# Block 1 in two groups of 256 tokens, the second computed in the expert slots of tiles 0 and 1

## The reference

```python
mod = (cond @ w_ada[l] + b_ada[l]).reshape(b, 6, d)
hn = modulate(rmsnorm(x, norm1_g[l]), shift1, scale1)
proj = hn @ w_in[l]
ya = dsa_attention(...)              # top 128 of the causal keys by an index score, softmax
yb = stick_breaking_attention(...)   # A[t,s] = beta_ts * prod_{s<j<t}(1-beta_tj), s < t
merged = sigmoid(ga) * (ya @ w_proj_a[l]) + sigmoid(gb) * (yb @ w_proj_b[l])
x = x + gate1[:, None, :] * (merged @ w_out[l])
hn2 = modulate(rmsnorm(x, norm2_g[l]), shift2, scale2)
# experts: top 16 of 128 x 128 sums of two key scores, for each token and head
pre = einsum('cd,chkd->chk', hc, u[ec]); coef = gc * gelu(pre)
f = einsum('chk,chkd->cd', coef, v[ec])
x = rmsnorm(x + gate2[:, None, :] * f, final_g)
x = second_block(x, meta_tokens_2, ...)
```

## Time and profile before

| | us |
|---|---|
| median of 3 runs (lowest, highest) | 2416.7 (2405.41, 2417.39) |
| span of the profiled execution | 2407.7 |
| first expert rows multiplied | 604.5 |
| token tile 0 summed | 939.4 |
| token tile 3 summed | 2032.8 |
| busy PE, DVE, ACT, POOL | 1877.5, 1439.3, 988.3, 574.0 |
| moved by DMA | 712.12 MB, 296 GB/s on average |

### The profile page before, as it was taken

How to read it: one execution, slowest core, us unless ns; L and a number is a source line. 1 busy time by engine, 2 the same in 40 slices (tenths; PEclk the granted TensorE clock), 3 DMA queues, 4 the chain that set the end, 5 groups by cost and what they waited for, 6 DMA issues and landing times.

```text
span 2407.7 us, 37910 instructions
## 1 busy us (share of the span) xinstructions
PE 1877.5 (78%) x14736; PEld 1182.7 (49%) x14736; DVE 1439.3 (60%) x3280; ACT 988.3 (41%) x2352; POOL 574.0 (24%) x554
## 2 busy tenths in 40 slices
PE   5998889999766644444435798988888885999999
PEld 3877457777333311100002453355666553677887
DVE  6747744554877677777777768765444333223554
ACT  3123545523443333333333576844444212343443
POOL 0000000001444444444344334443333331000000
PEclk8999999999887655555556897689999997999999
DMA  8932002233999999999999999999999996313565
GB/s 298 333 98 71 1 29 68 71 108 136 404 419 420 420 420 420 420 420 418 418 417 400 405 411 409 390 418 418 418 417 417 418 418 266 118 54 110 184 182 168
DMA packets 123616, 712.12 MB, mean 296 GB/s; under 512 B 14592, under 2 KB 15744, under 8 KB 57648
## 3 DMA queue, kind: packets, MB, share of 16 engines
q0 software_dynamic: 74608, 542.25, 54.6%
q1 hardware_dynamic: 48592, 167.33, 19.9%
q10 hardware_dynamic: 240, 0.16, 0.0%
HBM read 707.56 MB, written 2.13 MB: 295 GB/s over the span
## 4 chain that ended last, share of the span: by engine, by line
PE 46%; DMA 31%; DVE 10%; ACT 6%; issue 5%; POOL 2%; ACTq 0%; SPq 0%; DVEq 0%
DMA arena<-experts,eidx 30%; PE psum L718 9%; PE psum L719 8%; PE psum L720 8%; PE psum L1017 7%; DVE arena L1975 5%; POOL arena L1945 2%; PE psum L1308 2%; PE psum L1135 2%; ACT arena L1589 1%; PE psum L1185 1%; PE psum L1223 1%; ACT sq L1597 1%; PE psum L1259 1%; PE psum L1062 1%
## 5 line engine op out<-in xcount | busy, mean ns | idle before, releaser
L1975 DVE CUSTOM_DVE_ANT_0 arena<-arena 128x1024 f32<-128x1024 f32 x560 | 679.5, 1223 | 412.0 <-DMA arena<-experts,eidx 371.0
L1017 PE MATMUL psum<-arena,sq 32*32 32x512 f32 x8192 | 445.4, 842 | 449.4 <-ACT sq L1597 340.7
L1945 POOL DMA_INDIRECT arena<-experts,eidx x512 | 560.8, 1095 | 947.6 <-PE psum L1017 778.5
L1017 PEld LDWEIGHTS psum<-arena,sq 32*32 32x32 f32 x8192 | 95.1, 120 | 694.6 <-ACT sq L1597 500.5
L1583 ACT ACTIVATE arena<-arena 128x2 f32<-128x2 f32 x256 | 52.0, 203 | 736.5 <-DVE arena L1975 722.1
L718 PE MATMUL psum<-hn_high,w_high 128*128 128x512 f32 (+1 forms) x416 | 176.2, 424 | 15.4 <-DVE hn_low L1972 15.4
L720 PE MATMUL psum<-hn_high,ring_low 128*128 128x512 f32 (+1 forms) x432 | 175.2, 405 | 0.0
L719 PE MATMUL psum<-hn_low,w_high 128*128 128x512 f32 (+1 forms) x416 | 170.4, 410 | 0.0
L1330 PE MATMUL psum<-n_t,ring 128*128 128x256 f32 x704 | 164.3, 389 | 1.1 <-DVE n_t L1972 1.1
L1330 PEld LDWEIGHTS psum<-n_t,ring 128*128 128x128 f32 x704 | 132.5, 192 | 48.7 <-issue 30.1
L1597 ACT ACTIVATE sq<-sq,arena 128x32 f32<-128x32 f32 x512 | 136.9, 313 | 23.8
(11 more groups left out here) (327 smaller groups left out, 3102.1 us busy)
## 6 DMA issues: line engine op xcount, KB each, us to landing
ring<-w_stream SPq DMA_DIRECT2D x262, 512.0 KB
arena<-w_ada SPq DMA_DIRECT2D x48, 512.0 KB, 6.3
arena<-experts,eidx POOLq DMA_INDIRECT x512
arena<-cum_rows POOLq DMA_DIRECT2D x1, 2112.0 KB, 9.7
x<-xT SPq DMA_DIRECT2D x1, 2048.0 KB, 12.6
arena<-rel_rows POOLq DMA_DIRECT2D x1, 2048.0 KB, 15.3
arena<-sub_keys POOLq DMA_DIRECT2D x1, 1024.0 KB, 5.8
outT<-hn_rest SPq DMA_DIRECT2D x8, 128.0 KB
```

The costliest lines, as they stand in the source:

```text
L1017: last = mm(bank(4 + 2 * odd + a)[QUART * b:QUART * b + QUART, :], diag[k, s, :], rows[k, s, D + a * 512:D + (a + 1) * 512], start=c == 0, ...
L1945: nc.gpsimd.indirect_dma_start(rows[:, s, :], None, experts, bass.IndirectOffsetOnAxis(ap=eidx[:, n // P % 2, n % P:n % P + 1], axis=0)).t ...
L1975: return V.tensor_tensor_reduce(out=out, in0=a, in1=b, scale=1.0, scalar=0.0 if op1 == ALU.add else -TAKEN, op0=op0, op1=op1, accum_out=accum)
```

## The change

- **Group 1.** The first phase computes tokens 0 to 255 only. The dense products have 256 columns; stick breaking has 8 steps instead of 16, with the mask added as a product with `strict` on PE (DVE's `mask_out` and POOL's selects are gone), attention 8 steps with two gate tiles each. The copies of queries and keys out of PSUM go from DVE to ACT. One `w_ada` tile instead of two stands behind each dense tile, the last eight in the attention. POOL stores the early keys and values in HBM.
- **Group 2.** Tokens 256 to 511 are computed in `late_block`, a program of 251 ticks on PE, ACT and DVE, one tick in each slot of tile 0 and nine in eight slots of tile 1. All 78 weight tiles are streamed again, unsplit. The ring's order mixes them with the last ten query tiles of group 1 (`ring_order`). Early keys, values and the bias rows are loaded back in pieces by ACT's queue. The gates use tanh.
- The choices are spread evenly, twelve pieces in sixteen slots; query scores of tokens 256 to 511 come just before tile 2. The sums of tile 0 are turned in slots 150 and 158. The second block keeps its ticks.

```diff
+L_MEAN, L_ROOT, L_KI, L_WI, L_QI, L_IDX = 1, 6, 10, 14, 18, 21
+L_TOP = 39
+L_B, L_BH = 42, 6
+L_A, L_AS = 100, 4
+L_G, L_GM = 138, 6
+L_O = L_G + L_GM * KT
+L_N2 = L_O + 2 * KT + 4
+L_Q = L_N2 + 6
...
+L_DENSE = ([(L_KI, S_KI), (L_WI, S_WI)] + [(L_QI + 4 * m, QI + m) for m in range(4)]
+           + [(L_B - 8 + 2 * L_BH * p + 2 * j, (KB + p, QB + p, S_V + HP + p)[j]) for p in range(HP) for j in range(3)]
+           + [(L_A - 6 + 2 * L_AS * q + 2 * j, (KA + q, QA + q, S_V + q)[j]) for q in range(HP) for j in range(3)])
...
+def ring_order():
+
+    queries = [(4 * (j - LEAD), 0, S_WQ + j) for j in range(LEAD, 2 * PH)]
+    both = sorted(queries + [(t, 1, tile) for t, tile in L_DENSE])
+    return [(0, tile) for tile in range(S_WQ + LEAD)] + [(g, tile) for _, g, tile in both]
...
+def late_ticks(n):
+
+    return 1 + (n >= P and n % 8 == 0)
...
+                    last = product(bank(c, PAIR), part(ws[c], ALL, k), part(hn_parts, ALL, k),
+                                   k == 0, k == KT - 1)
...
+            def late_dense(n):
+                r, b = LATE_AT[n], late_bank(n)
+                if not S_GATE + KT <= n < S_PROJ:
+                    claim(b, "dense", n)
+                pe.wait_ge(ring_ready[r % SLOTS], 16 * (r // SLOTS + 1))
...
+                        last = mm(bank(b, PAIR, half), w[:, k, :], rhs[:, k, :], start=k == 0, stop=k == KT - 1)
...
+            def late_block():
+
+                for t in range(L_END):
...
+                    for shift, f in ((6, late_weighted), (3, late_sums), (0, late_z)):
+                        h = due(t, L_B + shift, L_BH, NH)
+                        if h is not None:
+                            f(h)
+                    for shift, f in ((8, late_values), (6, late_transposes), (0, late_scores)):
+                        st = due(t, L_A + shift, L_AS, 2 * HP)
...
+            def late_soft(h):
+                a = late_az[h % 2]
+                late_filled(act, "z", h, 2)
+                late_filled(act, "z", h, 3)
+                if h >= 2:
+                    late_filled(act, "yb", h // 2 - 1, h % 2)
+                act.preload_act_table_set("natural_log_exp_and_others")
+                steps(op(a, sticks, ACT.Abs))
...
             pair = block2(0)
+            late = late_block()
             for n in range(HEADS * PK):
...
+                for _ in range(late_ticks(n) if n < PAIR else 0):
+                    next(late, None)
                 for _ in range(pair_ticks(n)):
                     next(pair, None)
```

More of the change, by code:

```diff
@@ L347, in program @@
[L347 to L358, removed]
@@ L371, in program @@
[L371 to L380, removed]
@@ L381, in program @@
[L381 to L398, removed]
@@ new lines, in program, with small_one @@
+        rows = at(ROWS, SLOT, 2 * D)
+        free_small = [SMALL_AT]
+        def small_one(*shape):
+            n = 1
+            for s in shape:
+                n *= s
+            a = at(free_small[0], *shape)
+            free_small[0] += n
+            assert free_small[0] <= SC
+            return a
+        wgt = small_one(2, P)
+        pre = small_one(SLOT)
+        coef = small_one(SLOT)
+        half = small_one(2, NK)
+        top = small_one(2, PK)
+        topf = small_one(2, PK)
@@ L405, in program @@
[L405 to L418, removed]
-        pos2 = sb("pos2", [P, 2, PK], u32)
-        assert used[0] + 880 <= ARENA, used[0]
@@ new lines, in early_keys, with early_rows, late_rows @@
+            def early_keys(j):
+                late_emptied(pe, "early query", j)
+                claim(0, "key", j)
+                fill(key_products(j, 0, j), 0, "key", j)
+            def early_rows(a):
+                claim(0, "rows", 1, a)
+                fill(split_rows(1, range(4 * a, 4 * a + 4), lambda k: bank(0, P, k % 4 * P)), 0, "rows", 1, a)
+            def late_rows(n, a):
+                claim(2 + a, "rows", n, a)
+                for k in range(4 * a, 4 * a + 4):
+                    last = nc.tensor.transpose(bank(2 + a, P, k % 4 * P), n1[:, k, (n - 2) * P:(n - 1) * P], ident[:])
+                fill(last, 2 + a, "rows", n, a)
@@ new lines, in stick_products @@
+            def stick_products(h, b, stops):
+                p = h // 2
+                r = slice(64 * (h % 2), 64 * (h % 2) + 64)
+                tiles_of = (3, 2) if b == 2 else (1, 0)
+                for i in tiles_of:
+                    last = mm(stick(i), kbuf[p % 2][r, i * P:(i + 1) * P], qbuf[p % 2][r, max(0, i - 2) * P:PAIR],
+                              start=stops or i == tiles_of[0], stop=stops and b == 3)
+                    if b == 2 and stops:
+                        last = mm(stick(i)[:, 0:P], ident[:], strict[:], start=False, stop=True)
+                if b == 2 and not stops:
+                    for i in tiles_of:
+                        mm(stick(i)[:, 0:P], ident[:], strict[:], start=False, stop=False)
+                return last
@@ L1114, in last_rows @@
                                 last.then_inc(act_turned.sem, 1)
+                if g == 0:
+                    yield from ticks.until(3)
+                    for b in range(4):
+                        pe.wait_ge(late_free[b], late_uses[b])
                 for t in range(2):
@@ new lines, in late_weights, with late_y_out @@
+            def late_weights(h):
+                a = late_az[h % 2]
+                for b, first, last in ((2, 0, 3 * P), (3, 3 * P, 7 * P)):
+                    late_filled(act, "u", h, b)
+                    emptied(op(a[:, first:last], sticks[:, first:last], ACT.Exp), "z", h, b)
+            def late_y_out(e, p):
+                if e:
+                    late_filled(act, "yb", p, 1)
+                else:
+                    late_filled(act, "pv", p, 3)
+                emptied(op(late_y[e][:, p, :], bank(0, PAIR), ACT.Copy), *(("yb", p) if e else ("pv", p)))
```

1477 lines of the change are left out of this document (962 added, 515 removed).

## The result

The changed kernel takes 2499.7 us (median of 4 runs, 2482.5 to 2519.8), the kernel before 2412.8 us in the same comparison: a ratio of 1.034, 95% interval 1.031 to 1.038. Two executions are counted as slow, the one of 2519.8 us here and the one of 2318.3 us in experiment 2, and no ratio uses them. It is **slower by 3.4%** where 2320 us and a gain of 4% were forecast.

The account below looks back on a forecast made before the run. PE bounds the time before 604.5 us and the last stage, DMA the expert gathers between. 2407.7 - 259 + 108 + 55 = 2311.7 us of span, plus 9.0 for the median, gave 2320; range 2255 to 2395.

Parts of the forecast that it names:

- first phase shorter: Block 1 for the first 256 tokens alone: experts start at 345 us instead of 604.5, 259 us less.
- added bytes: Tiles 0 and 1: 45.1 MB of weights, keys, values and bias at 419 GB/s, unhidden, 108 us more.
- stalls in the slots: Tiles 0 and 1: engines waiting for each other beside the gathers, 55 us more, bounds 10 to 20 and 125.
- tiles 2, 3, last stage: Tiles 2 and 3 and the last stage keep their work: change 0, within 1% of before.
- far more than 3.3: Sign of a wrong prediction: stick-breaking slots in tile 0 taking far more than 3.3 us each.
- Dense tiles: First phase, after the first finished tile: 20 tiles of 2.85 us plus 5 us for w_ada tiles, 62 us.
- rival 2: First phase doesn't halve: late weights make a tile 3.6 us instead of 2.85, 45 us more, 2365 us; chance 0.10.
- Values: First phase, value tiles: 4 pairs of 5.6 us plus 4 us of ring wait, 27 us instead of 68.6.
- attention with gates: First phase: 8 steps of 9.5 us, set by ACT's chain, plus 6 us, 82 us instead of 133.3.
- the count of table loads: ACT in the slots gets 46 more table loads, 1.28 us each.
- Rival 1: Slots of tiles 0 and 1 hide everything but the added bytes: 2275 us; chance 0.25.
- Rival 3: Low PE clock bounds tiles 0 and 1: stalls of 90 us or more, 2498 us at clock 0.62; chance 0.20, 0.07 slower.

Follow-up runs that it names:

- experiment 2: Changed kernel with the second group's weight tiles still fetched but barely used; index, rounds, sticks, attention, gates, projections dropped: 2282.3 and 2318.3 us, no ratio given.
- experiment 1: Changed kernel without the second group's stick breaking and attention in the slots, outputs replaced by copies: 2340.4 us, ratio 0.970.
- experiment 12: Changed kernel with reordered TensorE steps, later score taking, wider-spaced heads and attention, later early-key products, and index products every second step: 2354.8 us, ratio 0.977.

## Why the prediction was wrong

The sum against what was measured, in us of span:

| step | forecast | measured | from |
|---|---|---|---|
| first phase shorter | -259 | -242 | first dots at 362.36 for 604.51 |
| added bytes | +108 | +119 | experiment 2, 773.1 against 653.7 |
| stalls in the slots | +55 | +195 | 967.7 against 773.1 |
| tiles 2, 3, last stage | 0 | +5 | 1154.8 against 1149.5 |
| span | 2311.7 | 2484.8 | |

**The failed step is "I take 55"**, the term of the sum for the stalls in the slots. They took 195 us, which its bounds of 10 and 125 didn't hold either. A slot of 40 to 95 took 4.5 us (252.29 for 56), where far more than 3.3 was named as the sign of being wrong. The 55 were worked out from busy time over a stretch (PE 110 us, DMA 102 us) with the nearest rows, where DMA kept 0.98 under heavy engines. But what decides here is not how full an engine is. It is how long a round trip through all of them takes, against the slots that it may last. That could have been added up. Some rows between VectorE's softplus at 592.76 and that of the next head at 623.92:

```profile
605.53 1.14 PE L1320 MATMUL psum<-arena,sq 32*32 32x512 f32 x32
606.60 3.72 PE L1167 MATMUL psum<-arena,ring 128*128 128x256 f32 x16
...
614.97 1.73 PE L1235 MATMUL psum<-arena 128*64 128x128 f32 x10
...
618.51 1.13 PE L1192 MATMUL psum<-arena 64*128 64x256 f32 x4
...
623.92 1.09 DVE L2469 SCALAR_TENSOR_TENSOR arena<-psum,arena 128x896 f32<-128x896 f32 x1 [15.22 <-ACT arena L1974]
```

The timelines show, one behind the other: table load back and diagonals 2.5 us, combine 2.2, sums 8.2, two combines 2.2, two weight tiles 7.4, values 1.7, products of the next head 3.0, table load and three functions 4.2. That is 31.4 us, and the two softplus stand 31.2 apart, against the 17.1 us that six slots take with the bytes alone (160.05 us for slots 40 to 95 in experiment 2). TensorE works for 24.7 of them, some of it at the low clock, then it pauses for the 6.7 us of ScalarE, and VectorE stands for 15.2. Over all eight heads the softplus come 30.0 us apart. Heads and attention steps together cost 175 us, by experiment 1. I had priced each at 5 us as the upper bound; the waits show 12.9 and 8.0 us on VectorE alone.

**The first phase** was 17 us too optimistic, by its own stages. Dense tiles took 74.6 us from the first finished one for 62: ScalarE waited 13 times for the ring's DMA, 30.7 us in all, so one of the 22 tiles was 3.4 us. That is rival 2's mechanism, and the rows show it in the dense stage only. Values took 41.4 for 27, and why is not followed up; the sticks took 43.6 for 42, attention with gates 74.0 for 82, and the rest 84.8 for 88.

**Bytes, tiles 2 and 3, the last stage, and the count of table loads** (204 for 158, 46 more) were right. Three slips in the working change little: eight heads of 5000 columns at 1.82 ns are 73 us of TensorE and not 67, the dense stage has 22 tiles, 21 of them behind the first, where 20 were priced, and the DMA shares behind the first stage are 0.04 to 0.31 in the earlier trace rows, not to 0.36.

**The rivals.** Rival 1 (2275, only the bytes) is near the kernel of experiment 2 (2282), which has little more than the weight tiles in the slots. The changed kernel isn't that. Rival 3 gave the right sign at 2498 us, but by the wrong cause: it wanted PE full at a clock under 0.8. In slots 40 to 95 the clock was 0.80 and PE was busy for 73% of the time. Its price for stalls of 90 us and more was the right size; I gave it 0.20, and 0.07 for a slower kernel, because I tied it to the clock.

## What to carry to other kernels

Work that is dealt out between the steps of a pipeline is priced by its round trips, not by its busy time. Write down for each hand-off which instruction of the pipeline stands ahead of it on each engine, add up the chain, and compare it with the slots it may last. If the chain is longer, place a producer ahead of the step on which its engine waits anyway, and a consumer behind the work that it would block; here two such edits and two more steps a head were worth 124 us with the same work and the same bytes. The two more steps left the heads as far apart (27.4 us for 27.2) and let eight slots pass between them instead of six, and the order was worth as much beside them as without them. Where no engine is full and a queue waits, look for the operation on which an engine stands with independent work behind it.

## What was new in the hardware

In some executions TensorE stays at its low clock through some 60 us in which it shows as busy throughout. Two windows around the stick breaking of the first phase, which is the same code in both kernels: first of the changed kernel, then of the kernel of experiment 12.

```profile
150.00:160.00 10.00, 8.86 (x67) 7.95 (x65) 9.45 (x26) 2.88 (x5) 0.00 (x0) 1.00 0.29 107
180.00:190.00 10.00, 10.00 (x56) 6.81 (x56) 3.70 (x10) 4.05 (x8) 0.00 (x0) 1.00 0.00 1
...
150.00:160.00 10.00, 8.04 (x59) 7.13 (x59) 9.36 (x29) 2.60 (x6) 0.00 (x0) 1.00 0.31 106
180.00:190.00 10.00, 10.00 (x34) 6.75 (x32) 3.70 (x10) 1.93 (x5) 0.00 (x0) 0.50 0.00 0
```

TensorE is busy for 10.00 of 10.00 us in both, but with a granted clock of 1.00 (2.4 GHz) and 56 matmuls here, and 0.50 (1.2 GHz) and 34 there. From 150 to 160 us both had 1.00. The first dots came at 389.89 and not at 362.36, 27 us later. The profile of experiment 1 has the same (0.50 from 180 to 190 us, first dots at 388.73), while the other ten experiments' profiles show 1.00 from 170 to 200 us as the changed kernel does, and the runs of experiment 12 fall into two groups, four at 2353 to 2356 us and two at 2376 and 2377. What decides between the two levels no row here shows. It stays open, and it is why the slots are counted from the first dots above.

A combine of two slots took 1.14 us in a busy stretch of the kernel after (605.53), less than the 1.26 us of the earlier trace rows, and 2.17 us at 595.22, behind a pause, as at the low clock there.
